# The last layer norm's third tile and half its fourth scaled on ScalarE, with the bias added on GpSimd

## What is computed

```python
def layer_norm(x, g, b):
    xf = x.astype(jnp.float32)
    mu = xf.mean(-1, keepdims=True)
    var = jnp.square(xf - mu).mean(-1, keepdims=True)
    return ((xf - mu) * lax.rsqrt(var + LN_EPS)).astype(x.dtype) * g + b

def layer(x, ...):
    x = layer_norm(ALPHA * x + 0.5 * swiglu(x, ffn1_w_up, ffn1_w_down), ln1_g, ln1_b)
    h, new_buf, S_new = mixer(x, ...)
    x = layer_norm(ALPHA * x + h, ln2_g, ln2_b)
    return layer_norm(ALPHA * x + 0.5 * swiglu(x, ffn2_w_up, ffn2_w_down), ln3_g, ln3_b), new_buf, S_new
```

## Time and profile before

| | us |
|---|---|
| three runs | 1793.74, 1793.78, 1794.19 |
| median | 1793.78 |
| span of the profiled execution | 1791.9 |
| TensorE busy in it | 1777.5 (99%) |
| VectorE busy | 1294.9 (72%) |
| ScalarE busy | 652.3 (36%) |
| GpSimd busy | 545.0 (30%) |

### The profile page before, as it was taken

The page is one execution under the profiler, slowest core; times in us unless marked ns, Lnnn a source line. Parts: engine busy times, 40 slices in busy tenths (PEclk is TensorE's granted clock), DMA queues, the critical chain, the costliest instruction groups (busy, mean ns, idle before and its releaser), DMA issues. The chain is left out here.

```text
span 1791.9 us, 26962 instructions
## 1 busy us (share of the span) xinstructions
PE 1777.5 (99%) x10852; PEld 1655.6 (92%) x10852; DVE 1294.9 (72%) x1704; ACT 652.3 (36%) x1110; POOL 545.0 (30%) x357
## 2 busy tenths in 40 slices
PE   9999999999999999999999999999999999999997
PEld 8989899898999999999997979798988989899896
DVE  7958485678788787776257776777867968485676
ACT  5425243243545454544106050514224325242343
POOL 2324232242232222121341323232243324233231
PEclk9999999999999999999999999999999999999999
DMA  7442423335443343422764948576963452324223
GB/s 273 130 141 71 140 73 130 126 98 177 147 148 127 113 135 98 143 87 92 269 235 140 335 171 304 203 278 220 346 252 139 130 152 85 130 79 133 91 86 106
DMA packets 87530, 283.65 MB, mean 158 GB/s; under 512 B 8688, under 2 KB 9072, under 8 KB 87152
## 3 DMA queue, kind: packets, MB, share of 16 engines
q1 hardware_dynamic: 47664, 171.79, 29.3%
q10 hardware_dynamic: 25200, 57.19, 9.0%
q0 software_dynamic: 14544, 52.96, 8.7%
HBM read 240.68 MB, written 42.28 MB: 158 GB/s over the span
## 5 line engine op out<-in xcount | busy, mean ns | idle before, releaser
L833 PE MATMUL ps<-th,wql 128*128 128x320 f32 x1136 | 351.4, 309 | 0.0
L833 PE MATMUL ps<-th,wqh 128*128 128x320 f32 x1136 | 351.2, 309 | 0.0
L833 PE MATMUL ps<-tl,wqh 128*128 128x320 f32 x1136 | 350.6, 309 | 0.0
L732 POOL TENSOR_TENSOR wl<-raw,wh 128x1024 fp32r<-128x1024 f32 x100 | 257.6, 2577 | 104.9 <-DMA wh<-in_weights 69.7
L1406 ACT ACTIVATE pu<-ps 128x320 f32<-128x320 f32 x213 | 93.3, 438 | 520.8 <-PE ps L833 520.7
L1850 DVE TENSOR_TENSOR wql<-qraw,wqh 128x512 fp32r<-128x512 f32 x213 | 260.9, 1225 | 17.3 <-ACT wqh L1406 17.1
L833 PE MATMUL ps<-xl,wqh 128*128 128x320 f32 x852 | 263.0, 309 | 0.0
L833 PE MATMUL ps<-xh,wqh 128*128 128x320 f32 x852 | 262.9, 309 | 0.0
L833 PE MATMUL ps<-xh,wql 128*128 128x320 f32 x852 | 262.8, 308 | 0.0
L745 POOL TENSOR_TENSOR quad_s<-qraw 128x512 f32<-128x512 f32 x71 | 94.0, 1324 | 476.5 <-DVE wql L1850 431.1
L1850 DVE TENSOR_TENSOR wql<-quad_s,wqh 128x512 fp32r<-128x512 f32 (+1 forms) x213 | 195.3, 917 | 44.8 <-ACT wqh L1406 44.1
(11 more groups left out here) (227 smaller groups left out, 3466.2 us busy)
## 6 DMA issues: line engine op xcount, KB each, us to landing
qraw<-in_quads SPq DMA_DIRECT2D x142, 512.0 KB, 3.6
raw<-in_weights SPq DMA_DIRECT2D x103, 512.0 KB, 3.8
wh<-in_weights POOLq DMA_DIRECT2D x94, 512.0 KB, 5.7
state<-in_state_ret ACTq DMA_DIRECT2D x32, 512.0 KB, 6.2
out_ret_sample<-state ACTq DMA_DIRECT2D x32, 512.0 KB, 4.4
state<-in_state_ret SPq DMA_DIRECT2D x16, 512.0 KB, 5.4
qk_scratch<-ctp SPq DMA_DIRECT2D x8, 640.0 KB, 5.6
swish_scratch<-ctp SPq DMA_DIRECT2D x6, 640.0 KB, 3.0
```

The costliest lines, as they stand in the source:

```text
L732: pool.tensor_tensor(w_lo(r), w_raw(r), w_hi(r).bitcast(f32), ALU.subtract).then_inc(chunk_split, 1)
L833: ins = nc.tensor.matmul(out, lhs, rhs, start=start, stop=stop, skip_group_check=adds)
```

## The change

The third tile, and columns 512 to 1023 of the fourth, are scaled on ScalarE, in two instructions that stand before the last tile's square and wait for a second count of `scaled`. GpSimd then adds the bias row in SBUF with two tensor_tensor instructions behind its accumulating stores, and counts them in a new semaphore `pool_done`. VectorE keeps the fourth tile's first 512 columns, behind a one-column memset that counts `scaled`. SyncE's stores are now four: the fourth tile's first half (after `y_done` 1), the third tile (`pool_done` 1), the fourth's second half (`pool_done` 2), the last tile's second half (`y_done` 3). ScalarE's own store waits for `y_done` 2, and the final wait counts five stores of this kind instead of four.

```diff
--- before.py
+++ after.py
@@ -28,6 +28,7 @@
 IDLE_START = 24
 LEVEL = 512
 ADDED = 2
+POOLED = ((ADDED, slice(0, 1024)), (ADDED + 1, slice(512, 1024)))
 LEAD = 1
 
 X_PIECES = [(half, range(k, k + 2)) for half in range(2) for k in range(0, KT, 2)]
@@ -493,8 +494,8 @@
         state_in = [sem(f"state_in{i}") for i in range(4)]
         state_out = [sem(f"state_out{i}") for i in range(4)]
         z_saved, y_out, conv_out, sp_out = sem("z_saved"), sem("y_out"), sem("conv_out"), sem("sp_out")
-        mean_made, scaled, y_scaled, y_biased, y_added, y_done = (
-            sem(n) for n in ("mean_made", "scaled", "y_scaled", "y_biased", "y_added", "y_done"))
+        mean_made, scaled, y_scaled, y_biased, y_added, y_done, pool_done = (
+            sem(n) for n in ("mean_made", "scaled", "y_scaled", "y_biased", "y_added", "y_done", "pool_done"))
         ones_made = sem("ones_made")
         block = ctx.enter_context(nc.Block())
 
@@ -698,10 +699,14 @@
             load_quad(2)
             load_quad(2)
             ffn(1)
-            for t in range(ADDED, TT - 1):
-                sync.wait_ge(y_done, t - ADDED + 1)
-                sync.dma_start(y_rows(t), y[:, t, :]).then_inc(y_out, 16)
-            sync.wait_ge(y_done, TT - ADDED + 1)
+            third, fourth = ADDED, ADDED + 1
+            sync.wait_ge(y_done, 1)
+            sync.dma_start(cols(0, 512, y_rows(fourth)), cols(0, 512, y[:, fourth, :])).then_inc(y_out, 16)
+            sync.wait_ge(pool_done, 1)
+            sync.dma_start(y_rows(third), y[:, third, :]).then_inc(y_out, 16)
+            sync.wait_ge(pool_done, 2)
+            sync.dma_start(cols(1, 512, y_rows(fourth)), cols(1, 512, y[:, fourth, :])).then_inc(y_out, 16)
+            sync.wait_ge(y_done, 3)
             sync.dma_start(cols(1, 512, y_rows(TT - 1)), cols(1, 512, y[:, TT - 1, :])).then_inc(y_out, 16)
             assert (ck.at, qk.at) == (CHUNKS, sum(QUAD_COUNT))
 
@@ -821,6 +826,9 @@
             for t in range(ADDED):
                 pool.wait_ge(y_scaled, t + 1)
                 pool.dma_start(y_rows(t), y[:, t, :], accum_op=ALU.add).then_inc(y_added, 16)
+            for n, (t, c) in enumerate(POOLED):
+                pool.wait_ge(y_scaled, ADDED + n + 1)
+                pool.tensor_tensor(y[:, t, c], y[:, t, c], lnb[:, c], ALU.add).then_inc(pool_done, 1)
 
 
         @block.tensor
@@ -1798,8 +1806,8 @@
                                             accum_out=mv[:, t, 1:2]))
                 squared.append(ad())
 
-            def scale(t):
-                nc.scalar.activation(y[:, t, :], y[:, t, :], ACT.Copy, scale=rt[:, 2, t:t + 1]).then_inc(y_scaled, 1)
+            def scale(t, c=slice(0, D)):
+                nc.scalar.activation(y[:, t, c], y[:, t, c], ACT.Copy, scale=rt[:, 2, t:t + 1]).then_inc(y_scaled, 1)
 
             nc.scalar.activation(rt[:, 1, TT:TT + 1], ones[:, 0:1].bitcast(f32), ACT.Sqrt)
             for t in range(ADDED):
@@ -1811,11 +1819,14 @@
             for t in range(ADDED, TT - 1):
                 square(t)
             roots(ADDED, TT - 1)
+            act.wait_ge(scaled, 2)
+            for t, c in POOLED:
+                scale(t, c)
             square(TT - 1)
             roots(TT - 1, TT)
-            act.wait_ge(y_done, TT - ADDED)
+            act.wait_ge(y_done, 2)
             act.dma_start(cols(0, 512, y_rows(TT - 1)), cols(0, 512, y[:, TT - 1, :])).then_inc(y_out, 16)
-            act.wait_ge(y_out, 16 * 4)
+            act.wait_ge(y_out, 16 * 5)
             act.wait_ge(y_added, 16 * ADDED)
             act.wait_ge(conv_out, 16)
             act.wait_ge(sp_out, 16 * H)
@@ -2288,8 +2299,8 @@
                         V.memset(rt[:, 3, TT:TT + 1], 0.0).then_inc(scaled, 1)
                 summed(0, TT - 1)
                 inv_deviation_of(range(ADDED, TT - 1))
-                for t in range(ADDED, TT - 1):
-                    scale_and_bias(t, (slice(0, D),))
+                V.memset(rt[:, 3, TT:TT + 1], 0.0).then_inc(scaled, 1)
+                scale_and_bias(ADDED + 1, (slice(0, 512),))
                 summed(1, TT - 1)
                 mean(TT - 1)
                 with_gain(TT - 1)
```

## The result

The changed kernel takes 1798.42 us (median of 9 runs, 1797.84 to 1798.99), the kernel before 1793.79 (9 runs, 1793.28 to 1794.47). The ratio is 1.0025, with a 95% interval of 1.0017 to 1.0033: slower by 4.6 us, where 0.7 was forecast and 1795.7 was the end of the range. The profiled execution's span went from 1791.9 to 1796.4.

A forecast was written before the change was run, and what follows sets the result against it. TensorE was taken to bound the kernel, leaving only the tail behind the last matmul to move. Earlier sum -1.68, centring held +1.90, root step held +0.46 gave +0.68 us: 1794.5, range 1792.0 to 1795.7.

The forecast's parts named there:

- What bounds: Whole kernel: TensorE busy 99% of the span; the change can move only the 9.3 us tail behind the last matmul.
- the sum's start: VectorE's second partial sum of the last tile: starts at 1782.69, 1.68 us earlier, as the two scalings become one half.
- ScalarE: Two added scalings, ending at 1783.24 and 1783.77, hold up the last tile's square by at most 0.1 us.
- The turns of GpSimd and VectorE: Two-input SBUF instructions alternate: GpSimd's additions hold centring and gain (+1.90 us) and the first one-column multiplication (+0.46 us).
- the second rival: Tail on VectorE: as forecast, but one-column multiplications pass unheld; +0.22 us, 1794.0; 12%.
- the first and third: Tail: turns don't bind, about 1792.2, 8%; or waits catch more or GpSimd starts later, 1795.3 or 1794.8, 16%.
- Stores: SyncE's four stores in fixed order: the earlier ones land hidden before the last, so splitting costs nothing.
- GpSimd is free: both accumulating stores are issued by 1778: GpSimd in the tail: idle after its two stores, so it can take the two bias additions.
- Nothing of GpSimd is left behind that: After the held first one-column multiplication: the remaining steps, half scalings and last store run at their old pace.
- The fourth rival: A new late thing of over 3.6 us: a GpSimd add taking twice its rows, with a store behind it; 2%.
- the 97% for no change: Chance given that the kernel's time stays within 0.2% (3.6 us) of the kernel before.

The follow-up runs named there:

- three stores: Kernel before with the third tile also scaled on ScalarE and added by a third accumulating store: 1795.63 against 1794.21; with the early drain 1794.95, ratio 1.0005.
- the early drain: One explicit GpSimd drain at about 1762, ahead of the accumulating stores; added to the kernel before: 1793.42 against 1793.52, ratio 0.9998.
- the last kernel: Three stores with the early drain, plus the fourth tile's second half scaled on ScalarE and added by a fourth accumulating store: 1798.82, ratio 1.0030.
- first probe: Kernel before plus a one-column GpSimd memset behind its accumulating stores, after VectorE's second y_done: 1794.49 against 1794.21, single run.
- the small program: Not the layer: GpSimd memsets, tensor_tensors and loads with explicit drains between; drains took 0.1 us more after one load, 0.7 after eight.

## Why the prediction was wrong

**What bounds, and the sum's start: right.** The sum was forecast at 1782.69, or 1782.60 with the shift of 0.09; it came at 1782.55, right behind the last matmul. The memset ran beside its neighbour and cost nothing, where I had put 0.03.

**ScalarE: right.** The third tile's scaling 1782.00 to 1783.15, the half to 1783.77 (0.71 us and not 0.63). The square began at 1783.67, some 0.15 us late, hidden behind VectorE's longer centring.

**The turns of GpSimd and VectorE: right, in mechanism and size.** GpSimd started 0.09 us after ScalarE and took 2.35. Centring took 3.13 (about 3.2 forecast) and ended at 1786.67 (1786.76 with the shift). The second addition is recorded with 2.24 and ended at 1787.79. The first one-column multiplication ran from 1787.20 to 1787.80, 0.60 us as forecast, so one-column instructions are held too, and the second rival falls with the first and third (the mean took 0.21 us). The rows that the prediction had for such instructions were fewer than it says: of the 45 multiplications in the earlier trace rows only 15 have one column. The two engines meet, then, not only at semaphores, as the description of the chip says, but also where both read SBUF. The last half scaling began at 1788.42, where 1788.61 was due. In all +0.49 where +0.68 stood: the 0.19 is that GpSimd's additions were each some 0.05 faster than the instructions they were costed by, and that centring and the multiplication ended a little sooner behind GpSimd's ends than forecast.

**Stores: right.** All landed before the last one, as the kernel without additions shows too.

**The step that failed** is none of the sum's terms but its frame: "GpSimd is free: both accumulating stores are issued by 1778", and, further on, "Nothing of GpSimd is left behind that". I took the end of the span to be the last store plus 2.4 us, as in the profile before, and asked of each engine only when its last instruction ends. GpSimd had its drain left: 8.3 us owed for 101 DMAs of the whole kernel, paid after its last addition, a term that the sum doesn't have. Before, it was over 1.8 us ahead of the others. The additions moved GpSimd's last instruction from 1777.84 to 1787.79, 10 us, and the end of the drain from 1789.86 to 1796.13, 6.3 us (before, the drain had also waited for the stores to land, as told below). The +0.5 of the engines and the 4.1 between ScalarE's arrival at 1792.07 and 1796.17 are the 4.6 of the runs. The fourth rival, with its 2%, had the place (a late thing on GpSimd) but neither this mechanism nor its price.

It could have been read. The rows of line 303 shown above were in the trace of the kernel before: a DRAIN of 13.1 us on an engine thought idle, ending 1.8 us before the end. That is all the slack that can be counted on for anything put behind GpSimd's stores. A bound from these rows (the DRAIN ends 12.0 us behind GpSimd's last DMA instruction, 1777.84) would have given 1787.8 + 12.0 = 1799.8 as an upper end, and 1789.9 as the lower.

**Chances.** 2% for slower by over 0.2% was far too low, and the 97% for no change rested on rivals that, but for the fourth, were all of one kind, the waits between VectorE and GpSimd. None asked what ends a program.

**Behind the stores.** Behind additions or memsets the drain is 0.083 us for each DMA. Behind the accumulating stores it was longer: 12.0 us after the last one's record in the kernel before, 13.0 with three stores. The landings sort this. The two stores of the kernel before, and of the same kernel with the early drain:

```profile
L823 POOL DMA_DIRECT2D out_y_prompt<-y x2: 898/972/1046, 1776.0 to 1776.8; - x2
DMA to landing us min/median/max: 5.6/7.3/8.9
...
L824 POOL DMA_DIRECT2D out_y_prompt<-y x2: 898/968/1038, 1775.4 to 1776.2; - x2
DMA to landing us min/median/max: 5.5/7.4/9.4
L303 POOLq DRAIN  x1: 9556/9556/9556, 1776.2 to 1776.2; - x1
```

In the kernel before, the second store lands at 1776.8 + 8.9 = 1785.7 and the drain ends at 1789.86, 4.2 us behind the landing. It is 4.2 us in the other two as well whose stores are GpSimd's last work and whose debt is unpaid: without the additions (landed at 1784.1, drain over at 1788.25) and with three stores (1789.1, 1793.3). That is half of the 8.3. With the debt paid early the drain ends right behind the landing: by 0.12 us with two stores (1785.6, 1785.71), 0.17 with three, 0.21 with four. One form fits the ends of the last drains of all twelve runs of the layer to 0.1 us: a first half of the debt, about 0.041 us for each DMA, runs from GpSimd's last instruction on; the second half, as long, starts when the first is over or when the last store has landed, whichever is later. It was fitted to these runs afterwards, and no run was made to test it.

**Left open.** Why a DMA that landed long ago costs the drain anything isn't shown. Nor is it whether its number or its bytes count: the one store of 256 KB, the fourth in the last kernel, added 0.04 us as those of 512 KB did, which speaks for the number, by one run.

## What to carry to other kernels

An engine is not free when its last instruction ends: ask the trace for the line that ends the program, and take the distance from the end of that engine's DRAIN to the arrival of the last of the others (1.8 us here) as the slack that is certain for anything put behind its last instruction. It can be more where the drain waits for a landing: the first probe's memset ended 6.8 us behind the last accumulating store's record and cost 1.2. Where GpSimd has issued many DMAs, that drain is long, and an explicit one in an earlier idle stretch pays it off. Work moved from VectorE to GpSimd as additions that read SBUF comes back as waits of VectorE where the two run side by side: here 3.6 us of GpSimd's additions took back all of the 1.7 us that they freed.

## What the runs showed of the hardware that was not expected

- GpSimd's DRAIN takes about 0.083 us for each DMA that GpSimd has issued since its last drain (8.34 us after 101, 8.2 after 99, 0.7 after 8, 0.1 after one), also when these have long landed: all but two were issued before 1753. Where the last DMA is still on its way, half of that (4.2 us for 101) comes behind its landing.
- The debt is paid once: the next drain, with only a memset in between, took 0.15 us, 0.10 of it the memset's.
- GpSimd's tensor_tensor of 128x1024 took 1.89 us in the small program, where both inputs were the same tile, and 2.35 to 2.39 in the layer, with two. Whether the second tile is the reason wasn't tried.
- With three and four accumulating stores in a row and plain stores beside them, all landed later: an accumulating one of 512 KB after up to 11.7 us (8.9 with two in a row), a plain one of 256 KB after 2.9 to 7 us instead of 2.0. Which slows which wasn't separated, and the spread is wide (9.7 and 11.7 us for the third store in two kernels that differ by the early drain).
